# The order in which a gather queue fetches its two kinds of rows across a tile's border

## The reference

```
hid = jnp.einsum('thkd,td->thk', expert_u[eid], xb)
act = jax.nn.gelu(hid, approximate=False) * gate
return jnp.einsum('thk,thkd->td', act, expert_v[eid])
```

## Time and profile before

| | us |
|---|---|
| median of 3 runs | 3541.54 |
| lowest and highest | 3536.38, 3543.12 |
| the profiled execution | 3535.6 |
| its span, first to last instruction | 3533.8 |

### The profile page before, as it was taken

The page is one execution under the profiler, slowest core; times in us unless marked ns, Lnnn a source line. Parts: engine busy times, 40 slices in busy tenths (PEclk is TensorE's granted clock), DMA queues, the critical chain, the costliest instruction groups (busy, mean ns, idle before and its releaser), DMA issues.

```text
span 3533.8 us, 37536 instructions
## 1 busy us (share of the span) xinstructions
PE 2612.1 (74%) x10985; PEld 1196.8 (34%) x10985; DVE 2230.6 (63%) x7062; ACT 1168.4 (33%) x3412; POOL 2140.7 (61%) x2069
## 2 busy tenths in 40 slices
PE   7997896785678667775786587757775678557877
PEld 5653343431343224322532243214321343113332
DVE  3125574666766866586668666777677766845543
ACT  2321233422342234323342334233422342223332
POOL 2202353555777677767776677667776777667663
PEclk9998898997889789977998798879898889778888
DMA  8115687888999999999999999999999999999995
GB/s 299 59 47 203 235 318 260 310 317 327 375 396 391 387 387 397 391 389 394 390 396 406 371 401 387 405 382 402 396 394 385 386 397 392 391 388 388 376 370 210
DMA packets 377540, 1227.83 MB, mean 347 GB/s; under 512 B 36296, under 2 KB 63992, under 8 KB 377208
## 3 DMA queue, kind: packets, MB, share of 16 engines
q0 software_dynamic: 294912, 1073.87, 78.5%
q1 hardware_dynamic: 79368, 141.94, 10.9%
q10 hardware_dynamic: 3056, 9.63, 0.7%
HBM read 1203.08 MB, written 22.21 MB: 347 GB/s over the span
## 4 chain that ended last, share of the span: by engine, by line
PE 31%; DMA 18%; POOL 18%; issue 17%; DVE 11%; ACT 5%; SPq 0%; POOLq 0%; DVEq 0%; ACTq 0%
PE bank L1117 15%; PE expert_sum L1117 14%; DMA v_rows<-in_peer_v_dram,expert_id 13%; POOL u_rows L666 9%; POOL v_rows L675 9%; DVE u_rows L2018 4%; DMA u_rows<-in_peer_u_dram,expert_id 4%; PE bank L1120 2%; ACT L705 1%; ACT weight_diagonals L705 1%; DMA w_query<-in_w_in_dram 1%; DVE arena L1965 1%; DVE arena L1971 1%; DVE arena L1974 1%; ACT arena L705 1%
## 5 line engine op out<-in xcount | busy, mean ns | idle before, releaser
L1117 PE MATMUL expert_sum<-v_rows,weight_diagonals 128*64 128x512 f32 x4096 | 1194.4, 717 | 567.3 <-issue 429.2
L2018 DVE CUSTOM_DVE_ANT_0 u_rows<-u_rows,ffn_in 128x512 f32<-128x512 f32 x2048 | 1309.7, 687 | 355.2 <-DMA u_rows<-in_peer_u_dram,expert_id 353.6
L666 POOL DMA_INDIRECT u_rows<-in_peer_u_dram,expert_id x1024 | 1053.0, 1028 | 642.6 <-issue 387.8
L675 POOL DMA_INDIRECT v_rows<-in_peer_v_dram,expert_id x1024 | 1040.5, 1016 | 535.9 <-issue 288.9
L1117 PEld LDWEIGHTS expert_sum<-v_rows,weight_diagonals 128*64 128x64 f32 x4096 | 320.6, 156 | 1251.6 <-issue 1240.8
L1117 PE MATMUL bank<-w_query,arena 128*128 128x512 f32 x576 | 286.6, 647 | 34.0 <-DMA w_query<-in_peer_w_query_dram 33.0
L705 ACT ACTIVATE weight_diagonals<-constants,expert_weight 128x64 f32<-128x64 f32 x1024 | 272.4, 336 | 8.3
L1117 PE MATMUL bank<-arena 128*128 128x128 f32 (+4 forms) x2176 | 247.7, 284 | 25.7 <-DVE arena L1778 13.1
L1117 PEld LDWEIGHTS bank<-arena 128*128 128x128 f32 (+3 forms) x2176 | 231.1, 191 | 83.4 <-issue 51.5
L1117 PE MATMUL bank<-w_out_sb,arena 128*128 128x512 f32 x512 | 226.5, 599 | 9.8 <-ACT arena L1083 6.5
L1120 PE MATMUL bank<-constants,arena 128*128 128x128 f32 x952 | 151.1, 301 | 108.7 <-DVE arena L1818 35.9
(11 more groups left out here) (194 smaller groups left out, 2052.2 us busy)
## 6 DMA issues: line engine op xcount, KB each, us to landing
w_query<-in_peer_w_query_dram SPq DMA_DIRECT2D x64, 1024.0 KB, 12.2
u_rows<-in_peer_u_dram,expert_id POOLq DMA_INDIRECT x1024, 7.5
v_rows<-in_peer_v_dram,expert_id POOLq DMA_INDIRECT x1024, 7.5
w_out_sb<-in_w_out_dram SPq DMA_DIRECT2D x2, 4096.0 KB, 18.7
w_query<-in_w_in_dram SPq DMA_DIRECT2D x12, 512.0 KB, 7.9
conv_scratch<-w_query SPq DMA_DIRECT2D x12, 384.0 KB, 6.8
arena<-conv_scratch SPq DMA_DIRECT2D x6, 768.0 KB, 5.0
tok_scratch<-token_out ACTq DMA_DIRECT2D x7, 648.0 KB, 3.0
```

The lines of the kernel that those rows point to most:

```text
L666: nc.gpsimd.indirect_dma_start(u_ring[:, j, :], None, table_u, bass.IndirectOffsetOnAxis(id_of(q, j), 0)).then_inc(u_landed[j], 16)
L675: nc.gpsimd.indirect_dma_start(v_ring[:, j, :], None, table_v, bass.IndirectOffsetOnAxis(id_of(q, j), 0)).then_inc(v_landed[j], 16)
L1117: return nc.tensor.matmul(out_, lhsT, rhs, start=start, stop=stop, **kw)
L2018: last = v.tensor_tensor_reduce(u_ring[:, j, half], u_ring[:, j, half], xb[:, j % NB, half], 1.0, 0.0, ALU.mult, ALU.add, hid_half[:, q % ...
```

## The change

The block at the border goes. In every period each u pair has the v pair n - 6 ahead of it, the border's periods too. The wait for the new numbers stands behind the period's first v pair and before its first u pair, and the one in period `EARLY` moves to the same place.

```
-                late = e > 0 and g == 0
-                if late:
-
-                    for n in range(q * PAIRS - VLAG, q * PAIRS):
-                        gather_v_pair(n)
-                if q == 0 or q == EARLY or late:
-
-                    pool.wait_ge(ids_ready, 1 if q == 0 else e + 2)
-                    pool.sem_inc(wait_carrier)
                 for pair in range(PAIRS):
-                    if not (late or q and g == 1 and pair < VLAG - PAIRS and q > NG):
-                        gather_v_pair(q * PAIRS + pair - VLAG)
+                    gather_v_pair(q * PAIRS + pair - VLAG)
+                    if pair == 0 and (q == EARLY or g == 0):
+
+                        pool.wait_ge(ids_ready, e + 2 if q else 1)
+                        pool.sem_inc(wait_carrier)
                     gather_u(q, pair)
```

## The result

| | median us | lowest to highest | ratio to before, 95% interval |
|---|---|---|---|
| before | 3540.3 | 3536.4 to 3543.1 | |
| the change | 3518.0 | 3516.9 to 3522.4 | 0.9937 (0.9918 to 0.9956) |

The change makes the kernel 22.3 us faster, 0.63%. The forecast was 3532.6 us, a gain of 8.9, in a range from 3522 to 3543: the direction was right, the size 2.5 times too small, and the time lies 4 us under the range. One execution of a later kernel ("v wait away") took 13235 us where its ten others took 3524 to 3537, and is left out of that kernel's ratio.

The account below looks back on a forecast made before the run. The gathers' data path was taken to bound the kernel. Regained idle DMA of 8.9 us at seven borders, with 0 for the `EARLY` wait, took the median from 3541.5 to 3532.6 us, range 3522 to 3543.

Parts of the forecast that it names:

- What bounds the kernel: Whole run: the gathers' data path sets the pace, 2.56 us a pair, with GpSimd's issue hardly faster at 2.5 us.
- The two waits: GpSimd at the second border: waits for PE at v-2 (1.19 us) and DVE at u+5 (1.32 us) go, 1.9 us gained.
- The price of the border: Seven 40 us windows behind borders: DMA share short of 1.03 means 8.9 us idle in all, 1.3 a border; 8.9 taken.
- The upper end: Over seven borders: GpSimd's 1.9 us lead at each, its surplus filling later gaps, gives at most 13 us.
- The other side: Tile's end: v-1 lands 12.8 us later, DVE idles some 2 us for it, yet goes on 2.0 to 2.5 us sooner.
- (A): Behind borders: GpSimd's slow gathers, 2.7 us a pair, starve DMA, not its waits; 0 to 3 us gained, 3540; chance 0.18.
- (B): Border gathers slow beside busy DVE, 1057 against 941 ns, 9 us over seven borders, eating the gain; 3541.5; chance 0.08.
- (C): Tile's closing product on v-1 ends after 1272.9, delaying the next tile 3.5 us; 3558 or 3545; chance 0.10.
- (D): GpSimd's and DVE's lead of 1.9 to 2.5 us a border stays whole, 15 us gained; 3526; chance 0.14.

Follow-up runs that it names:

- v wait away: Changed kernel with each border ordered v-6 v-5 v-4, u+0, v-3 v-2 v-1, u+1 to u+5, and `EARLY` as before; ratio 0.9982 to the kernel before.
- lag 7 at the border: Changed kernel with each v pair 7 pairs behind in place of 6 for u+0 to u+6 of each border; ratio 0.9934 to the kernel before.
- lag 8 at the borders: Changed kernel with each v pair 8 pairs behind in place of 6 for u+0 to u+7 of each border; ratio 1.0021 to the kernel before.

## Why the prediction was wrong

**What bounds the kernel: right.** The data path of the gathers sets the pace behind the first tile. The kernels whose queue was kept fuller at the borders, and that left the rest alone, were faster by about the bytes regained there.

**The two waits: right.** Both went as forecast at the second border, with no wait for the expert numbers (14 us of margin) and none for the new rows. DVE's idle time ahead of u+0 was forecast as 2.6 us and is 2.47; v+0 behind v-6 as 31 and is 31.8.

**The price of the border: this step failed.** It took the idle of the DMA engines from their share, "8.9 us of idle DMA in all", and called it the most that could return at the borders. The rows had the other number beside it: 366 to 387 GB/s where 409 is full, which is 19.7 us. The share is the time that packets took. With the queue thin a packet takes longer in the mean: between 1257 and 1282 of the trace before, a gather's packets of 4 KB took 176 ns, against 163 between 1170 and 1200. It is a tail that does it, as the middle one fell from 162 to 159 ns while one in twenty took over 220 in place of 169. So the engines showed a share of 0.99 and moved a tenth less (369 GB/s of 409). "Short" by the share is 8.9 us, by bytes 19.7, and the time measured fell by 22.

**The upper end: too low as well.** It was seven times GpSimd's 1.9 us at the second border, 13 us. That border was among the mild ones: from v-6 to v+0 GpSimd took 35.1, 33.3, 33.5, 35.1, 33.6, 32.9 and 44.2 us at the seven before, and 31.3 to 31.8 at the first six and 34.4 at the seventh now, 24 us less in all. Not all of that counts: 9.9 of the 24 are the seventh border's, where GpSimd's long wait before fell while the queue was still full (410 GB/s from 3094 to 3110), and the run gained only 1.4 us behind it. Still, one place was worked out in full and multiplied, where the seven had to be looked at.

**The other side: right in its outcome, wrong in its working.** The closing product was expected at 1268.4 to 1270.4 in the old count; it came at 1269.0 to 1272.6, as PE's clock was at its lower level there. The granted clock is 0.50 from 1258 to 1266.7, the 1.2 GHz level, behind a stretch at 0.72 in which PE was busy 3.01 of 8 us; in the kernel before the same product ran at 1.00, the 2.4 GHz level, behind a stretch in which PE was busy 8.99 of 10 us. So DVE stood 4.92 us for it in place of 2, and the next tile's front leads by 0.3 us in place of 2.0. That cost nothing that these runs show: with lag 7 at the border both come later still, and the time is the same.

**The rivals.** (A), that GpSimd's slow gathers keep the queue thin, fell: at 1.03 and 410 GB/s the queue is full though gathers beside a busy DVE are still slow (1045 ns for u between 1251 and 1284). (B) fell with it. Between 1228 and 1261 the means are 1039 and 992 ns, against 941 in the old block:

```profile
L675 POOL DMA_INDIRECT v_rows<-in_peer_v_dram,expert_id x13 | 13.5, 1039 | 4.0 <-issue 3.7 <-PE expert_sum L1111 0.3
L666 POOL DMA_INDIRECT u_rows<-in_peer_u_dram,expert_id x12 | 11.9, 992 | 3.7 <-issue 3.7
```

So the slowing is there, as the rule of the Trainium skill ("GPSIMD Engine Reference", "Key points") has it, and it doesn't thin the queue here: v-6 to v+0 takes 31.8 us for twelve pairs, 2.65 a pair against the 2.56 of the data path, and the work queued ahead covers the difference of 1 us. (C) stood nearer than the time shows: the product ended at 1272.6 where 1272.9 was its limit, and DVE stood 4.92 us where over 5 was its sign. But lag 7 goes beyond both and loses nothing, so the limit was put in the wrong place; at lag 8 lateness costs, by another path. (D), more than the forecast, was nearest; its 3526 rested on the same 1.9 us, and was still 8 us off.

What stays open: every kernel of the table but lag 8 at the borders gained 1 to 5 us more than "short" gives, the one with only `EARLY` moved too (-2 us, not told from none), and lag 8 lost 3 more. A small gain of `EARLY`'s can't be the whole of it, since four of these kernels have that wait as before. It could be what the windows leave out behind their end, or that "short" comes from one execution of each.

## What to carry to other kernels

When a queue of transfers sets the pace, measure a gap in bytes against the full rate, not by the busy share: a thin queue looks nearly full. Here a ring of four filled in a run of six stalled at the ring's end, and two rings taken in turn, or in runs of three, didn't. And where a fixed queue stands for one consumer, look at what stands behind in it that is free to go: putting it ahead at that place can fill the stall. Here 12 us came of the 29 reckoned, as part was lost again further on.

## What the runs showed of the hardware

- A gather's 4 KB packets took 163 ns in the mean with a full queue (409 GB/s) and 176 ns with a thin one (369 GB/s); the middle one took 162 and 159 ns, and 95 of 100 took under 169 and 220 ns. The share of busy time went from 1.03 only to 1.01 where the rate went from 409 to 385 GB/s.
- PE's granted clock fell from 1.00 to 0.50 at the tile's closing product when the same products came spread out, and the product then took 3.68 us in place of 1.94.
